# A hybrid decoder trunk on one core: the mixer's slots in another order, the first loads and the last norm rebuilt

## The reference

```
x = x + 0.5 * swiglu_ffn(rmsnorm(x, norm_ffn1), w_ffn1_in, w_ffn1_out)      # hidden width 2816
u = rmsnorm(x, norm_mix);  q,k,v,g,p,c,gates = split(u @ w_in)
y_ret  = (retention(q, k, v) * silu(g)) @ w_ret_out        # 4 heads of 128, rotary, rms norm per head
y_pool = pool_mixer(p, w_pool) * pool_scale                # causal means over 2, 4, 8, 16 tokens
y_conv = silu(layernorm(causal_depthwise_conv31(a * sigmoid(b)))) @ w_conv_out
gates  = sigmoid(gates + gate_bias)                        # three gates of 1024
x = x + (gates0 * y_ret + gates1 * y_pool + gates2 * y_conv) @ w_out
x = x + 0.5 * swiglu_ffn(rmsnorm(x, norm_ffn2), w_ffn2_in, w_ffn2_out)
```

## Time and profile before

| | |
|---|---|
| runs | 1203.64 us median of 3 (1203.62 to 1203.89) |
| profiled execution | 1203.59 us, span 1201.8 us |
| TensorE | busy 1169.2 us (97%) |
| VectorE | busy 756.2 us (63%) |
| ScalarE | busy 533.8 us (44%) |
| GpSimd | busy 46.0 us (4%) |
| granted TensorE clock | 0.993 of full speed on average |
| mixer of layer 0, layer 1 | about 209 to 415 us, and about 799 to 1005 us |
| first product, last product | 11.62 us, 1194.33 us |

### The profile page before, as it was taken

How to read it: one execution, slowest core, us unless ns; L and a number is a source line. 1 busy time by engine, 2 the same in 40 slices (tenths; PEclk the granted TensorE clock), 3 DMA queues, 4 the chain that set the end, 5 groups by cost and what they waited for, 6 DMA issues and landing times.

```text
span 1201.8 us, 13278 instructions
## 1 busy us (share of the span) xinstructions
PE 1169.2 (97%) x5360; PEld 965.0 (80%) x5360; DVE 756.2 (63%) x903; ACT 533.8 (44%) x586; POOL 46.0 (4%) x73
## 2 busy tenths in 40 slices
PE   6999999999979999999999999999999799999997
PEld 4888888888868888888888888888888688888886
DVE  5554455798988665454465545367989967554542
ACT  7444345543444454443364443364424355444331
POOL 3000000100000010000010000010000001000000
PEclk9999999999989999999999999999999899999999
DMA  8654355543634455445554545555337444554440
GB/s 328 250 210 174 142 213 207 194 164 114 237 149 175 158 194 210 159 157 210 210 214 171 211 142 202 185 206 196 130 115 266 151 176 166 202 209 158 158 175 35
DMA packets 33661, 220.02 MB, mean 183 GB/s; under 512 B 3760, under 2 KB 4144, under 8 KB 8640
## 3 DMA queue, kind: packets, MB, share of 16 engines
q1 hardware_dynamic: 31104, 212.09, 48.1%
q0 software_dynamic: 1648, 6.06, 1.4%
q10 hardware_dynamic: 848, 1.02, 0.3%
HBM read 218.10 MB, written 1.05 MB: 182 GB/s over the span
## 4 chain that ended last, share of the span: by engine, by line
PE 90%; DVE 7%; ACT 1%; DMA 1%; issue 0%; SPq 0%; POOL 0%; DVEq 0%; POOLq 0%; ACTq 0%
PE acc L302 28%; PE acc L304 28%; PE acc L303 28%; PE tr L360 3%; DVE w_lo L884 3%; DVE y L1066 2%; DMA raw<-in_weights 1%; ACT w_hi L599 1%; DVE ua L1115 0%; PE tr L451 0%; PE tr L461 0%; DVE gates L1086 0%; DVE sideT_lo L1174 0%; DVE sideT_lo L1092 0%; ACT v L731 0%
## 5 line engine op out<-in xcount | busy, mean ns | idle before, releaser
L884 DVE TENSOR_TENSOR w_lo<-raw,w_hi 128x2048 fp32r<-128x2048 f32 (+2 forms) x207 | 451.2, 2212 | 107.9 <-ACT w_hi L599 107.2
L599 ACT CAST w_hi<-raw 128x2048 fp32r<-128x2048 f32 (+2 forms) x207 | 380.3, 1849 | 253.9 <-PE acc L304 251.7
L302 PE MATMUL acc<-w_hi,xT_hi 128*128 128x512 f32 x1184 | 472.7, 399 | 9.7 <-DVE w_lo L890 4.7
L304 PE MATMUL acc<-w_hi,xT_lo 128*128 128x512 f32 x1184 | 463.0, 391 | 0.0
L303 PE MATMUL acc<-w_lo,xT_hi 128*128 128x512 f32 x1184 | 461.9, 390 | 0.0
L302 PEld LDWEIGHTS acc<-w_hi,xT_hi 128*128 128x128 f32 x1184 | 223.0, 188 | 55.6 <-issue 6.7
L304 PEld LDWEIGHTS acc<-w_hi,xT_lo 128*128 128x128 f32 x1184 | 222.6, 188 | 48.0
L303 PEld LDWEIGHTS acc<-w_lo,xT_hi 128*128 128x128 f32 x1184 | 223.3, 189 | 43.1
L937 DVE SCALAR_TENSOR_TENSOR h<-acc,rs,silu_gate 128x256 f32<-128x256 f32 x88 | 42.5, 483 | 222.9 <-ACT silu_gate L643 222.9
L302 PE MATMUL acc<-w_hi,hT_hi 128*128 128x512 f32 x352 | 137.8, 392 | 0.0
L304 PE MATMUL acc<-w_hi,hT_lo 128*128 128x512 f32 x352 | 137.1, 389 | 0.0
(11 more groups left out here) (104 smaller groups left out, 557.0 us busy)
## 6 DMA issues: line engine op xcount, KB each, us to landing
raw<-in_weights SPq DMA_DIRECT2D x195, 1024.0 KB, 4.8
raw<-in_weights SPq DMA_DIRECT2D x8, 512.0 KB, 3.5
bias<-in_gate_bias POOLq DMA_DIRECT2D x6, 512.0 KB, 7.6
raw<-in_weights SPq DMA_DIRECT2D x8, 256.0 KB, 3.6
scale_row<-in_pool_scale POOLq DMA_DIRECT2D x2, 512.0 KB, 9.5
out<-x SPq DMA_DIRECT2D x4, 256.0 KB, 2.1
x<-in_x ACTq DMA_DIRECT2D x3, 256.0 KB, 7.7
band<-in_band POOLq DMA_DIRECT2D x1, 768.0 KB, 8.9
```

The costliest lines, as they stand in the source:

```text
L302: nc.tensor.matmul(o, a_hi, b_hi, start=first, stop=False)
L304: return nc.tensor.matmul(o, a_lo, b_hi, start=False, stop=last)
L599: nc.scalar.copy(w_hi[:, hf % HIGHS, 0:n], raw[:, hf % RAWS, 0:n]).then_inc(hi_split, 1)
L884: nc.vector.tensor_tensor(w_lo[:, hf % RAWS, 0:n], raw[:, hf % RAWS, 0:n], w_hi[:, hf % HIGHS, 0:n].bitcast(F32), ALU.subtract).then_inc(l ...
```

## The change

Five groups of edits:

- **VectorE's slots.** In each slot the reading of accumulators (gates, merges) comes before the taps, and the taps are spread anew: 4, 6, 14, 16, 16, 10, 16, 14, 14, 8 and the rest (before 4, 7, 14, 15, 12, 10, 8, 18, 6, 10, 10 and the rest). `retained` moves to the end of the slot before the pool product, ahead of `gate_z(POOLED, 1, 1)`.
- **ScalarE's slots and the layer norm.** In the gate slots a cast comes before the tanh. `ln_apply` moves from VectorE to ScalarE, as scale x y + shift; GpSimd computes the shift with two more operations per t. TensorE's `turn_ret(1)` comes half a block earlier, `turn_y` and `turn_yn(0)` later in their blocks.
- **GpSimd.** The head norm comes before the wait for the pool gate and the load of the retention bias.
- **The start.** The eight gains of the first norm come with ident in one transfer; par comes later, from ScalarE's queue after the first x_high. The second half comes in two parts of 512 KB and is cast and subtracted in quarters. The last two quarters of x are issued by SP behind those weights, and turned two steps and one step later. The first square moves behind x_high. TensorE multiplies zeros (14 matmuls of 512 columns, bf16) while it waits for the first data.
- **The end.** Mean squares are taken per 512 columns, half_rs is left out, x is multiplied by norm_final before the factor is known, and then the two halves are scaled at the same time on ScalarE and VectorE, and stored from two queues.

```diff
-        ident = sb("ident", [P, P])
+        ident_gain = sb("ident_gain", [P, P + 32])
+        ident = ident_gain[:, 0:P]
-        ring_at = -(-arena_from // 32) * 32
+        ring_at = -(-arena_from // 128) * 128
...
+        weighted = gates
...
-                in_block(l, g0, 0, norm, {1: lambda: turn_x(l, norm, 1, 0),
-                                          4: lambda: turn_x(l, norm, 1, 1)})
+                in_block(l, g0, 0, norm, {3: lambda: turn_x(l, norm, 1, 0),
+                                          5: lambda: turn_x(l, norm, 1, 1)} if l + f == 0 else
+                         {1: lambda: turn_x(l, norm, 1, 0), 4: lambda: turn_x(l, norm, 1, 1)})
...
-                in_block(l, M_GATE_RET, 0)
-                in_block(l, M_GATE_RET, 1, mid={3: lambda: turn_ret(l, 0)})
-                in_block(l, M_GATE_RET + 1, 0, mid={3: lambda: turn_ret(l, 1)})
+                in_block(l, M_GATE_RET, 0, mid={3: lambda: turn_ret(l, 0),
+                                                6: lambda: turn_ret(l, 1)})
+                in_block(l, M_GATE_RET, 1)
+                in_block(l, M_GATE_RET + 1, 0)
...
-                in_block(l, M_GATE_CONV, 1, mid={3: lambda: turn_y(l, 0), 5: lambda: turn_y(l, 1)})
+                in_block(l, M_GATE_CONV, 1, mid={5: lambda: turn_y(l, 0), 7: lambda: turn_y(l, 1)})
...
-                in_block(l, M_GATE_CONV + 1, 1, mid={1: lambda: turn_yn(l, 0),
+                in_block(l, M_GATE_CONV + 1, 1, mid={2: lambda: turn_yn(l, 0),
...
+            def keep_busy(n):
+                warm = scale_row[:].bitcast(BF16)
+                for _ in range(n):
+                    nc.tensor.matmul(ret[:, 0, :], warm[:, 0:P], warm[:, 0:NB], start=True, stop=True)
+            pe.wait_ge(warm_set, 1)
+            keep_busy(6)
             pe.wait_ge(ident_landed, 16)
             turn_x(0, 0, 0, 0)
+            keep_busy(2)
             turn_x(0, 0, 0, 1)
+            keep_busy(6)
... SP
+            for i in (0, 1):
+                s = slice(i * D, (i + 1) * D)
+                sp.dma_start(raw[:, 1, s], half_in(1)[:, s]).then_inc(first_landed[4 + i], 16)
+            for c in (0, 1):
+                sp.dma_start(x[:, 1, columns(c)], x_part(1, c)).then_inc(x_landed[1][c], 16)
... ScalarE
+            def ln_apply(l, t):
+                name = ("y", l, t)
+                act.wait_ge(ln_shift_ready, l * T + t + 1)
+                nc.scalar.activation(pin[:, t, :], bank(name), ACT.Identity,
+                                     bias=ln_shift[:, t:t + 1], scale=ln_rstd[:, t:t + 1]
+                                     ).then_inc(tr_taken[TURN[name] % 2], 1)
...
+                ln_apply(l, 0)
+                ln_apply(l, 1)
                 conv_silu(l, 0)
... ScalarE, first block
                 x_high(l, norm, 1, 1)
+                if l == 0 and norm == 0:
+                    square(l, norm, 0)
+                    for hf in (2, 3):
+                        cast(hf)
                 cast(l * HALVES + 2 * g + 4)
... VectorE, mixer
                 gate_z(l, POOLED, 0, 1)
                 subs(M_GATE_POOL + 1)
-                conv_taps(l, 18)
                 gate_z(l, POOLED, 1, 0)
+                conv_taps(l, 16)
+                retained(l, 0)
+                retained(l, 1)
 
                 gate_z(l, POOLED, 1, 1)
                 merge_first(l, 0, 0)
...
                 subs(M_POOL)
-                conv_taps(l, 6)
-
-                retained(l, 0)
-                retained(l, 1)
+
                 subs(M_GATE_RET)
-                conv_taps(l, 10)
                 side_low(l, ("ret", l, 0), (slice(None), slice(None), tokens(0)), HEADS, 3)
                 gate_z(l, RET, 0, 0)
+                side_low(l, ("ret", l, 1), (slice(None), slice(None), tokens(1)), HEADS, 4)
+                conv_taps(l, 14)
 
                 gate_z(l, RET, 0, 1)
                 subs(M_GATE_RET + 1)
-                side_low(l, ("ret", l, 1), (slice(None), slice(None), tokens(1)), HEADS, 4)
-                conv_taps(l, 10)
                 gate_z(l, RET, 1, 0)
+                conv_taps(l, 14)
 
                 gate_z(l, RET, 1, 1)
                 subs(M_RET)
-                conv_taps(l, CH * TAPS)
                 merge(l, RET, 0, 0, merged_ret)
                 merge(l, RET, 0, 1, merged_ret)
+                conv_taps(l, 8)
 
                 merge(l, RET, 1, 0, merged_ret)
                 merge(l, RET, 1, 1, merged_ret)
+                conv_taps(l, CH * TAPS)
                 subs(M_GATE_CONV)
                 gate_z(l, CONV, 0, 0)
...
-                sub(l * HALVES + 2 * (M_GATE_CONV + 1) + 3)
-                for t in range(T):
-                    ln_apply(l, t)
-                sub(l * HALVES + 2 * (M_GATE_CONV + 1) + 4)
+                subs(M_GATE_CONV + 1)
                 gate_z(l, CONV, 1, 0)
... GpSimd, behind ln_rstd, for each t
+                    nc.gpsimd.tensor_tensor(ln_minus[:, t:t + 1], ln_mean_var[:, t, 0:1],
+                                            small[:, 4:5], ALU.mult).then_inc(ln_negated, 1)
+                    pool.wait_ge(ln_rstd_ready, l * T + t + 1)
+                    pool.wait_ge(ln_negated, l * T + t + 1)
+                    nc.gpsimd.tensor_tensor(ln_shift[:, t:t + 1], ln_minus[:, t:t + 1],
+                                            ln_rstd[:, t:t + 1], ALU.mult).then_inc(ln_shift_ready, 1)
```

More of the change, by code:

```diff
@@ L131, in trunk @@
         half_rs = sb("half_rs", [P, T])
+        end_small = sb("end_small", [P, 5, T])
+        end_meansq = end_small[:, 0:2, :]
+        end_eps, end_total, end_rs = (end_small[:, i, :] for i in range(2, 5))
         head_sumsq = sb("head_sumsq", [P, T, HEADS])
@@ L243, in trunk, with gain @@
         uses = [[0, 0] for _ in range(T)]
+        def gain(l, norm, k):
+            if l == 0 and norm == 0:
+                return ident_gain[:, P + k:P + k + 1]
+            return par[:, l, PAR_GAIN[norm] + k:PAR_GAIN[norm] + k + 1]
         def tokens(t):
@@ L609, in x_high @@
                     k = 4 * c + i
-                    col = PAR_GAIN[norm] + k
                     nc.scalar.activation(xT_hi[:, k, tokens(t)],
                                          bank(("x", l, norm, t, c))[:, i * P:(i + 1) * P],
-                                         ACT.Copy, scale=par[:, l, col:col + 1]
+                                         ACT.Copy, scale=gain(l, norm, k)
                                          ).then_inc(x_hi_ready, 1)
@@ L802, in mixer @@
                 head_squares(l, 1)
+                cast(ahead(M_GATE_POOL + 1) + 1)
                 gate_tanh(l, POOLED, 1, 0)
-                cast(ahead(M_GATE_POOL + 1) + 1)
+                cast(ahead(M_POOL))
                 gate_tanh(l, POOLED, 1, 1)
-                cast(ahead(M_POOL))
                 cast(ahead(M_POOL) + 1)
@@ L825, in mixer @@
                 cast(ahead(M_GATE_CONV))
+                cast(ahead(M_GATE_CONV) + 1)
                 gate_tanh(l, CONV, 0, 0)
-                cast(ahead(M_GATE_CONV) + 1)
                 cast(ahead(M_GATE_CONV + 1))
                 gate_tanh(l, CONV, 0, 1)
+                ln_apply(l, 0)
+                ln_apply(l, 1)
                 conv_silu(l, 0)
@@ L849, in mixer @@
                 finish(l, 3, ahead(M_OUT + 1))
-            act.wait_ge(par_landed, 16)
+            act.wait_ge(ident_landed, 16)
             x_high(0, 0, 0, 0)
+            act.dma_start(par[:], params.rearrange("l p n -> p l n")).then_inc(par_landed, 16)
             cast_first(0)
+            cast_first(1)
             x_high(0, 0, 0, 1)
-            for i in range(1, 4):
+            for i in range(2, 8):
                 cast_first(i)
-            cast(1)
-            square(0, 0, 0)
-            cast(2)
-            cast(3)
             for l in range(L):
@@ L869, in _ @@
                 ffn(l, 1, (l + 1, 0) if l + 1 < L else None)
-            square(L, 0, 0)
-            square(L, 0, 1)
+            for t in range(T):
+                for n in (0, 1):
+                    wait_acc_taken(act, L - 1, FFN2 + FB, t, n)
+                    nc.scalar.activation(squares[:, columns(n)], x[:, t, columns(n)], ACT.Square,
+                                         scale=D ** -0.5, accum_out=end_meansq[:, n, t:t + 1]
+                                         ).then_inc(end_meansq_ready, 1)
+                act.wait_ge(end_rs_ready, t + 1)
+                act.wait_ge(end_weighted, 2 * t + 1)
+                nc.scalar.activation(weighted[:, t, columns(0)], weighted[:, t, columns(0)],
+                                     ACT.Copy, scale=end_rs[:, t:t + 1]).then_inc(out_ready[0], 1)
+                act.wait_ge(out_ready[0], t + 1)
+                act.dma_start(out.rearrange("a (t p) d -> p (a t) d", p=P)[:, t, columns(0)],
+                              weighted[:, t, columns(0)]).then_inc(stored, 16)
         @block.vector
         def _(dve):
-            for i, value in enumerate((-0.5, EPS, 0.5, 1.0 / DH)):
```

(19 more changed lines are left out.)

132 lines of the change are left out of this document (75 added, 57 removed).

## The result

The changed kernel takes **1196.03 us** (median of 4 runs, 1194.38 to 1197.01), the kernel before 1203.66 (1203.62 to 1203.89): ratio 0.9934, interval 0.9923 to 0.9946, 7.6 us faster. The runs now spread over 2.6 us, before over 0.3. The profiled execution is the slowest of the four, 1197.01 with a span of 1194.9.

The account below looks back on a forecast made before the run. TensorE, busy 97% of the span, was taken as the bound, so its waits and low clock set the price. -5.4 (start) -5.1 (mixers) -1.45 (end) = -11.95 on 1203.59: 1192 us, own range 1189 to 1195, stated range 1185 to 1198.5.

Parts of the forecast that it names:

- The start, -5.4: Start of the kernel: earlier first product (8.15) brings turn_h from 33.42 to 28.0, -5.4 us.
- a net 0.7: Start: if the warm-up doesn't hold the clock, first products cost 1.6 more, turn_h's wait shrinks 0.9; -4.7 for -5.4.
- The order in the gate slot: Mixer: gate_z(1,0) before taps idles VectorE 2.6 us; new pool product wait 2.45; the 5.3 wait on gate_z(RET,1,0) goes.
- the 1.9 us priced: Mixer after the pool product: TensorE's waits at a w_lo half 0.75, a merge 0.55, the next 0.3, last tap 0.3.
- VectorE's queue up to the conv norm: Mixer: from 316.5 VectorE has 50.8 us of available work, so gate_z(CONV,0,0) starts at 367.35, before 368.16.
- GpSimd behind the subs: Conv norm: w_lo subs hold GpSimd's t=1 chain, ln_apply(1) ends at 376.1, turn_yn(0) waits 3.2 us.
- Rival 1: Conv norm: GpSimd's chain isn't held, CONV starts 3.0 us sooner per layer, 1186 us; chance 0.22.
- -2.6 per layer, -5.1: Conv norm: CONV product starts at 380.8 instead of 383.37, 2.6 us sooner per layer, 5.1 in both.
- rival 2: New waits lower the clock, 1.9 to 3.2 us per fall; 1196 to 1198, or 1200; chance 0.22.
- The end, -1.45: End: split squares, no half_rs and parallel scaling bring the end from 1201.8 to 1200.35, -1.45 us (1.0 to 1.7).
- Rivals 3 and 4: 3: Identity makes ScalarE load tables, 1197, chance 0.04; 4: shifted arrays slow operand reads, 1211 at 4 ns, chance 0.05.
- the one with four falls: Version of rival 2: clock falls twice at the conv norm and at the pool product as well, 1200 us.

Follow-up runs that it names:

- e1: Changed kernel with one wait added: VectorE waits for the layer norm's shift of t=1 before its next two w_lo subs; 1186.59 us.
- e4: The changed start and end with the mixer of before on all engines; 1197.13 us.
- e6: e5 with taps spread once more: eight before and five behind the first pool gate, 6 and 7 around the third; 1181.18 us.
- e5: e1 with, in addition, six of 16 taps moved in front of gate_z(POOLED,1,0); 1182.09 us.
- e7: Changed kernel with the layer norm's apply back on VectorE between the two subs, without GpSimd's two extra operations per t; 1188.53 us.
- e3: Changed kernel with 14 bf16 matmuls, result unused, put ahead of turn_yn(0), where TensorE waits; 1192.93 us.
- e8: e1 without the 14 warm-up matmuls at the start; 1187.82 us.

## Why the prediction was right, and where not

- **The start, -5.4.** Measured -5.7 at the first transpose of h, -5.6 at the mixer. The prediction took the old time there as 33.42, from the view of the chain that ended last; on the timeline, by which the rest is read, it is 33.26, so its own steps gave -5.3. The first product came 0.3 later than worked out (8.43 for 8.15), but the wait at `turn_h` was 0.5 and not 0.9, as VectorE was through with `hidden(0,1)` at 27.49 and not at 27.9. That the warm-up holds the clock was right; without it the start loses 1.3 us, where the prediction had a net 0.7. The gain isn't the same in every execution: with the same start the first transpose of h is at 27.42 to 27.64 in e1 to e4 and e6, but at 28.29 in e5 and 28.08 in e7, where TensorE waited 0.78 and 1.02 us for x.
- **The order in the gate slot.** Right in place and size: VectorE idle 2.56 (2.6), wait at the pool product 2.30 (2.45), `gate_z(RET,1,0)` without a wait. What it left out is that the clock falls there, in both layers. That cost little in the balance: TensorE was late for the next w_lo half, merge and tap by the 1.7 us that 3.4 us at half the clock cost, and so didn't wait at them for the 1.9 us priced (0.75, 0.55, 0.3, 0.3). M_GATE_CONV started at 353.32 on the old axis, worked out 352.95. e1, with a low stretch there in layer 0 alone, shows the size: from the pool product's restart to M_GATE_CONV 36.01 us in layer 0 and 35.53 in layer 1.
- **VectorE's queue up to the conv norm.** The sum of 50.8 us gave gate_z(CONV,0,0) at 367.35; measured 361.70, on the old axis 367.33.
- **GpSimd behind the subs.** Right: 2.33 and 2.48 for two operations beside two subs, `turn_yn(0)` waiting 3.49 for 3.2 predicted. Rival 1, by which the chain slips through, is refuted by this row, and e1 shows its cause. The Trainium skill ("GPSIMD Engine Reference", 1. Specifications) speaks of contention against VectorE instructions with two SBUF inputs. For the w_lo subs the traces agree, 0.55 against 2.48. Taps have two such inputs as well, and by the rule the head norm would now be slowed too. It is, but by little: its three operations took 0.34, 0.32 and 1.77 us beside the taps, and 0.22, 0.20 and 1.67 before, beside operations that read `acc`. Taps last 0.4 us each, subs 2.2, and e7's power, begun 0.2 us ahead of a sub, took only 0.55. Both fit a hold that lasts until the VectorE instruction already running is over; that is argued and not shown, as no run tried subs cut short.
- **The step that failed: the conv norm's "-2.6 per layer, -5.1".** Measured +0.2 in layer 0 and -0.6 in layer 1 in the profiled execution, and -1.1 for both layers between medians (e4). The working went from `turn_yn(0)` (372.9 and 3.2 of wait, 376.1) to the CONV product at 380.8 at full pitch, 4.7 us; it took 7.2 in layer 0, because the clock fell inside the wait. With the clock held up by e3 the same way took 4.70. The prediction held this as rival 2 with 1196 to 1198 and a chance of 0.22, and left it out of the sum although it had itself read a fall after 2.3 us of idleness in the earlier trace rows and forecast a wait of 3.2. A wait longer than one that is seen to lower the clock had to be priced with its fall in the forecast. The remaining 0.4 us in layer 0 come in before it: `turn_yn(0)` at 370.92 is 376.55 on the old axis, as GpSimd's chain ended 0.2 later than worked out (370.01, 375.64 on the old axis, for 375.4) and ScalarE's apply took 0.78 us for 0.65 to 0.7.
- **The runs' spread of 2.6 us.** It was not predicted. Only one execution of each kernel has a trace, but every run has its mean granted clock: 0.992, 0.992, 0.994 and 0.995 for 1197.01, 1196.28, 1195.78 and 1194.38 us. So the clock is the likely source. In the profiled executions a low stretch in the changed mixer is 3.4 or 6.8 us long, and the same pool wait of 2.3 us lowered the clock in both layers (changed kernel, e3, e8) or in one (e1, e7). The landing of x at the start is a second source: e5, whose clock is 1.00 through both mixers, still spreads over 0.8 us. e6 spreads over 0.2.
- **The end, -1.45.** Measured -0.9. From the last add's start to the store's issue it took 3.20 us, worked out 3.1 (ScalarE's scaling took 0.72, not 0.6). From the issue to the span's end it took 2.95, where 2.5 was taken over from before. The store on ScalarE's queue took 2.5 us from issue to landing, that on SP's 2.1, as before. Whether that lies in the queue or in the second store running beside it is open: no run sent them one at a time.
- **Rivals 3 and 4.** `Identity` loaded no table, and the pitch is still 0.227 (ten starts from 304.78 to 306.82): both refuted. The Trainium skill ("ScalarE: Activation LUTs", Table sets: the hidden batching unit) has identity in every set; the trace agrees, with one load in the whole execution at 1.67 us.

In sum: -5.6 for -5.4, mixers -0.4 for -5.1, end -0.9 for -1.45. The sign, the waits and their places were right; the size failed mainly by one term, the clock. That 1196.03 still lies in the range is luck in part: the range was wide enough to take in rival 2, and of that rival's two versions the one with four falls, which is what happened, said 1200. It was cheaper because falls at the pool product cost nothing by the mixer's end (e1: 201.37 us with and without; e7: 202.14 without in layer 0, 202.13 with in layer 1) and the one at layer 1's conv norm cost 1.5 us.

## What to carry to other kernels

When a chain of small operations runs on GpSimd beside long VectorE instructions and its end is awaited by the bounding engine, it can pay to let VectorE wait for the chain: here 1.3 us of wait in each of two layers gained 9.4 us in all; look in the trace for small operations that end just behind a long one of VectorE's. Price a wait of TensorE with the low clock that follows it, in the forecast itself, as soon as it is as long as one after which the trace shows a fall, and then ask whether TensorE sets the time behind it: if another engine does, the slow matmuls are hidden. And where an order is rewritten, ask of each instruction moved forward whether its input is there: the idle time in front of it is paid again by whatever stands behind it, unless independent work is put in front.
